# A head's output held in one PSUM bank, copied first in its step, transposed two steps later; a third bank for the transposes

## What is computed

```python
for layer in range(DEPTH):                       # 2
    h = _rmsnorm(x, mix_norm_gain[layer])
    q, k, v, conv_in = split(h @ w_in[layer])
    attn = _dilated_attention(rope(norm(q)), rope(norm(k)), v)   # 8 heads
    u = silu(layernorm(causal_dwconv(a * sigmoid(g))))           # 31 taps, 512 channels
    x = x + concat([attn, u]) @ w_out[layer]
    x = x + ffn(rmsnorm(x))                      # two matrix products and 3 taps
```

## Time and profile before

| | us |
|---|---|
| median of 3 runs | 2470.47 (2468.65 to 2470.99) |
| the profiled execution | 2470.12 |
| its span, first to last instruction | 2467.8 |
| attention steps of layer 0 | about 251 to 411 of the span |
| attention steps of layer 1 | about 1477 to 1636 of the span |

### The profile page before, as it was taken

How to read it: one execution, slowest core, us unless ns; L and a number is a source line. 1 busy time by engine, 2 the same in 40 slices (tenths; PEclk the granted TensorE clock), 3 DMA queues, 4 the chain that set the end, 5 groups by cost and what they waited for, 6 DMA issues and landing times.

```text
span 2467.8 us, 30567 instructions
## 1 busy us (share of the span) xinstructions
PE 2396.0 (97%) x11672; PEld 1956.5 (79%) x11672; DVE 1575.8 (64%) x1511; ACT 803.8 (33%) x1066; POOL 166.0 (7%) x57
## 2 busy tenths in 40 slices
PE   7999888999999999999999998899999999999999
PEld 6888667888888888888778876678888888888887
DVE  5999775566555555555749997746655555555555
ACT  4322665432222222222332237644322222222221
POOL 0222001100000000000103120011000000000000
PEclk9999999999999999999999999999999999999999
DMA  4334531111111111111112254301121111111111
GB/s 157 86 86 127 120 71 31 47 52 52 52 51 51 42 51 42 51 47 46 42 35 77 77 154 94 78 10 52 45 66 35 51 51 51 51 42 51 42 51 68
DMA packets 46674, 153.42 MB, mean 62 GB/s; under 512 B 7424, under 2 KB 10112, under 8 KB 46592
## 3 DMA queue, kind: packets, MB, share of 16 engines
q1 hardware_dynamic: 45728, 149.93, 21.1%
q10 hardware_dynamic: 864, 2.36, 0.2%
HBM read 131.02 MB, written 21.23 MB: 62 GB/s over the span
## 4 chain that ended last, share of the span: by engine, by line
PE 88%; issue 5%; DVE 4%; ACT 2%; POOLq 0%; DMA 0%; DVEq 0%; POOL 0%; SPq 0%; ACTq 0%
PE mm L436 59%; PE aux L436 19%; PE aux L572 3%; PE mm L548 3%; PE aux L591 3%; DVE y L1118 1%; DVE sc L1244 1%; PE aux L463 1%; ACT pT_large L882 0%; PE aux L472 0%; ACT sc L868 0%; DMA x<-xT 0%; POOLq L1421 0%; DVE x_lo L1060 0%; PE aux L529 0%
## 5 line engine op out<-in xcount | busy, mean ns | idle before, releaser
L436 PE MATMUL mm<-x_hi,w_hi 128*128 128x512 f32 x1952 | 609.3, 393 | 16.1 <-DVE x_lo L1060 11.6
L436 PE MATMUL mm<-x_hi,w_lo 128*128 128x512 f32 x1952 | 604.5, 391 | 0.0
L436 PE MATMUL mm<-x_lo,w_hi 128*128 128x512 f32 x1952 | 604.2, 391 | 0.0
L436 PEld LDWEIGHTS mm<-x_hi,w_hi 128*128 128x128 f32 x1952 | 363.9, 188 | 95.6 <-issue 11.9
L436 PEld LDWEIGHTS mm<-x_lo,w_hi 128*128 128x128 f32 x1952 | 367.0, 188 | 79.6
L436 PEld LDWEIGHTS mm<-x_hi,w_lo 128*128 128x128 f32 x1952 | 367.0, 188 | 78.8
L735 ACT ACTIVATE w_hi<-w_raw 128x1024 fp32r<-128x1024 f32 x154 | 162.0, 1058 | 654.7 <-PE mm L436 458.1
L1118 DVE SCALAR_TENSOR_TENSOR y<-u_pad,cpar,y 128x1024 f32<-128x1024 f32 x240 | 313.3, 1338 | 3.4 <-ACT y L788 2.6
L1054 DVE TENSOR_TENSOR x<-x,aux 128x1024 f32<-128x1024 f32 x176 | 214.8, 1221 | 120.4 <-PE aux L436 109.9
L1048 DVE TENSOR_TENSOR w_lo<-w_raw,w_hi 128x1024 fp32r<-128x1024 f32 x154 | 192.5, 1256 | 54.5 <-ACT w_hi L735 50.2
L1066 DVE TENSOR_TENSOR uv<-mm,rinv 128x1024 f32<-128x1024 f32 x44 | 53.9, 1225 | 220.1 <-PE mm L436 219.9
(11 more groups left out here) (185 smaller groups left out, 2897.1 us busy)
## 6 DMA issues: line engine op xcount, KB each, us to landing
w_raw<-weights SPq DMA_DIRECT2D x188, 512.0 KB, 3.6
qk_scratch<-m SPq DMA_DIRECT2D x64, 128.0 KB, 2.1
qk_scratch<-o SPq DMA_DIRECT2D x64, 128.0 KB, 2.1
x_hi<-qk_scratch SPq DMA_DIRECT2D x32, 256.0 KB, 6.3
q_first<-qk_scratch SPq DMA_DIRECT2D x8, 512.0 KB, 4.8
k_hh_first<-qk_scratch SPq DMA_DIRECT2D x16, 256.0 KB, 6.3
k_ll_first<-qk_scratch SPq DMA_DIRECT2D x16, 256.0 KB, 6.9
x_hi<-qk_scratch SPq DMA_DIRECT2D x8, 512.0 KB, 4.7
```

What stands on the lines that cost most here:

```text
L436: last = pe.matmul(acc[:, cols], a, b[:, cols], start=start and n == 0, stop=stop and n == 2)
```

## The change

ScalarE's copy of a head's output stands first in step 8h + 11 and no longer last. The transpose back moves from step 8h + 12 to 8h + 14, and in its step it now stands behind the product with v. The "o" fills move from the steps 23 and 25 to 24 and 26. As the output is copied earlier, all heads can use one bank (`o_bank`, the upper half of `stat_s`), and the lower half joins the two banks of `stat_b` as a third for the transposes. So fill f goes to bank f % 3 and waits for fill f - 3. One step is added to the end, a quarter of the first output product moves with it, and the sum over the convolution's channels that follows now waits for all three banks before its first half.

```diff
-O_AT = 23
+O_AT = 24
+H_AT = 14
@@
-        if n >= 12 and (n - 12) % TB == 0 and n < STEPS + 12:
-            fills.append((n, "h", (n - 12) // TB, None, None))
+        if n >= H_AT and (n - H_AT) % TB == 0 and n < STEPS + H_AT:
+            fills.append((n, "h", (n - H_AT) // TB, None, None))
@@
+TURN_BANKS = 3
+BANK_FILLS = [len(range(b, PT, TURN_BANKS)) for b in range(TURN_BANKS)]
@@
+        turn_bank = [stat_b[:, 0:BANK], stat_b[:, BANK:], stat_s[:, 0:BANK]]
+        o_bank = stat_s[:, BANK:]
@@
+        def bank_read(l, f, after=0):
+            return at(l, BANK_FILLS[f % TURN_BANKS], f // TURN_BANKS + 1 + after)
@@ turn
-                    bank = stat_b[:, f % 2 * BANK:(f % 2 + 1) * BANK]
-                    pe.wait_ge(pt_read[f % 2], at(l, PT // 2, f // 2 + 1))
+                    bank = turn_bank[f % TURN_BANKS]
+                    pe.wait_ge(pt_read[f % TURN_BANKS], bank_read(l, f))
+                    if f == 2:
+                        pe.wait_ge(v_turned, at(l, PAIRS, PAIRS))
@@ attend
-                    if k == 0 and (l or h >= 2):
-                        pe.wait_ge(o_moved, at(l, HEADS, h - 1))
+                    if k == 0 and (l or h):
+                        pe.wait_ge(o_moved, at(l, HEADS, h))
@@ PE, a step
-                        if FILLS[f][0] == n and FILLS[f][1] in "ph":
+                        if FILLS[f][0] == n and FILLS[f][1] == "p":
                             turn(f)
                     ...
-                        if FILLS[f][0] == n and FILLS[f][1] == "o":
+                        if FILLS[f][0] == n and FILLS[f][1] in "ho":
                             turn(f)
@@ PE, behind the steps
                 pe.wait_ge(y_summed, at(l, CT - 1, CT - 1))
+                for bank in range(TURN_BANKS):
+                    pe.wait_ge(pt_read[bank], at(l, BANK_FILLS[bank], BANK_FILLS[bank] + 1))
                 for half in range(2):
-                    pe.wait_ge(pt_read[half], at(l, PT // 2, PT // 2 + 1))
@@ ACT, a step
+                    if n >= 11 and (n - 11) % TB == 0 and n < STEPS + 11:
+                        move_out((n - 11) // TB)
                     ...
                     if n < STEPS:
                         exps(n)
-                    if n >= 11 and (n - 11) % TB == 0:
-                        move_out((n - 11) // TB)
```

More of the change, by code:

```diff
@@ L76 @@
 STEPS = HEADS * TB
-O_AT = 23
+O_AT = 24
+H_AT = 14
 BLOCKS = (0, 6, 1, 7, 2, 4, 3, 5)
 ATTENDS = ((5, 0), (6, 3), (9, 1), (10, 2))
-LAST_STEP = STEPS + 10
+LAST_STEP = STEPS + 11
 DOWN = GROUPS * KT
@@ L141 @@
 PT = len(FILLS)
-assert PT % 2 == 0
+TURN_BANKS = 3
+BANK_FILLS = [len(range(b, PT, TURN_BANKS)) for b in range(TURN_BANKS)]
 LAST_FILL = [max(i for i, f in enumerate(FILLS) if f[1] == "p" and f[2] == n) for n in range(STEPS)]
@@ L284, in trunk @@
         pt_full = sem("pt_full"); o_moved = sem("o_moved")
-        pt_read = [sem(f"pt_read{i}") for i in range(2)]
+        pt_read = [sem(f"pt_read{i}") for i in range(TURN_BANKS)]
         step_done = sem("step_done")
@@ L580, in attend @@
                         pe.wait_ge(v_turned, at(l, PAIRS, PAIRS))
-                    if k == 0 and (l or h >= 2):
-                        pe.wait_ge(o_moved, at(l, HEADS, h - 1))
-                    for bank in range(2):
-                        fills = [f for f in range(LAST_FILL[h * TB + at_step - 3] + 1) if f % 2 == bank]
-                        pe.wait_ge(pt_read[bank], at(l, PT // 2, len(fills) + 1))
-                    cols = slice(hh * BANK + pair * P, hh * BANK + (pair + 1) * P)
+                    if k == 0 and (l or h):
+                        pe.wait_ge(o_moved, at(l, HEADS, h))
+                    last_fill = LAST_FILL[h * TB + at_step - 3]
+                    for f in range(max(0, last_fill + 1 - TURN_BANKS), last_fill + 1):
+                        pe.wait_ge(pt_read[f % TURN_BANKS], bank_read(l, f, 1))
+                    cols = slice(pair * P, (pair + 1) * P)
                     for kb in range(2 * pair + 2):
@@ L590, in attend @@
                             if kb <= 2 * pair + half:
-                                last = pe.matmul(stat_s[half * HEAD_DIM:(half + 1) * HEAD_DIM, cols],
+                                last = pe.matmul(o_bank[half * HEAD_DIM:(half + 1) * HEAD_DIM, cols],
                                                  vp[b][:, kb, hh * HEAD_DIM:(hh + 1) * HEAD_DIM],
@@ L611, in _ @@
                         out_part(0, 0, [0], 0)
-                    if n == STEPS + 5:
+                    if n == STEPS + 7:
                         out_part(0, 0, [1], 0)
@@ L723, in _ @@
             act.sem_inc(pt_read[0], 1)
+            act.sem_inc(pt_read[2], 1)
             for t in range(0, KT, 2):
@@ L882, in read_turn @@
                         act.activation(pT(which)[:, a:z, :], bank[:, 0:(z - a) * P].rearrange(
-                            "p (k q) -> p k q", q=P), ACT.Copy).then_inc(pt_read[f % 2], 1)
+                            "p (k q) -> p k q", q=P), ACT.Copy).then_inc(pt_read[f % TURN_BANKS], 1)
                     else:
@@ L886, in read_turn @@
                         act.activation(o_nat[:, a * 4:(a + 1) * 4, :], bank.rearrange("p (b c) -> p b c", c=P),
-                                       ACT.Copy).then_inc(pt_read[f % 2], 1)
+                                       ACT.Copy).then_inc(pt_read[f % TURN_BANKS], 1)
                 def move_out(h):
@@ L892, in move_out @@
                     act.wait_ge(o_read, at(l, HEADS, h + 1))
-                    act.activation(o_turned[h % 2], stat_s[:, h % 2 * BANK:(h % 2 + 1) * BANK], ACT.Copy
+                    act.activation(o_turned[h % 2], o_bank, ACT.Copy
                                    ).then_inc(o_moved, 1)
                 for n in range(LAST_STEP):
+                    if n >= 11 and (n - 11) % TB == 0 and n < STEPS + 11:
+                        move_out((n - 11) // TB)
                     for f in range(PT):
@@ L1251, in read_turn @@
                         return
-                    fills = [g for g in range(f + 1) if g % 2 == f % 2]
-                    dve.wait_ge(pt_read[f % 2], at(l, PT // 2, len(fills) + 1))
+                    dve.wait_ge(pt_read[f % TURN_BANKS], bank_read(l, f, 1))
                     out = (slice(None), which, slice(a * BANK, (a + 1) * BANK))
@@ L1265, in read_out @@
                     dve.tensor_tensor(o_nat[:, :, hh * HEAD_DIM:(hh + 1) * HEAD_DIM],
-                                      stat_b[:, f % 2 * BANK:(f % 2 + 1) * BANK].rearrange("p (b c) -> p b c", b=TB),
+                                      turn_bank[f % TURN_BANKS].rearrange("p (b c) -> p b c", b=TB),
                                       row_rec.unsqueeze(2).broadcast_to([P, TB, HEAD_DIM]),
                                       ALU.mult).then_inc(o_read, 1)
-                    dve.drain().then_inc(pt_read[f % 2], 1)
+                    dve.drain().then_inc(pt_read[f % TURN_BANKS], 1)
                 step_taps = list(STEP_TAPS)
@@ L1282, in _ @@
                             read_turn(f)
-                    if n >= 12 and (n - 12) % TB == 0:
-                        read_out((n - 12) // TB)
+                    if n >= H_AT and (n - H_AT) % TB == 0 and n < STEPS + H_AT:
+                        read_out((n - H_AT) // TB)
                 def out_add(u, parts=range(2)):
```

## The result

The changed kernel takes 2448.07 us in the median of four runs (2444.03 to 2449.60), the kernel before 2470.73 beside it. The ratio is 0.9907, with a 95% interval of 0.989 to 0.9924: faster by 0.9%, within the stated range, at the price of the first rival and not of the forecast of 2437. One execution among all the runs of this text, the fourth of `turn_late`, took 3154.33 us at a granted clock of 0.705 and is set aside.

The account below looks back on a forecast made before the run. TensorE, busy 97% of the span, was taken as the bound, with waits in attention. Per layer 14.9 + 4.1 - 3 x 0.5 - 0.6 = 16.9 us, 33.8 in two, from 2470.1: forecast 2437 us, range 2427 to 2453.

Parts of the forecast that it names:

- the first rival: Clock still falls at boundaries behind step 11, so 11.6 us of the gain is lost: 2449 us, chance 0.20.
- the case that I gave 0.60: The forecast itself: copy waits gone and clock full in the attention steps, 2437 us.
- The waits for the copy go: TensorE's 14 waits for the copy of a head's output, 28.2 us in both layers, were to vanish.
- Heads 1 to 6 save 14.9 us, less 1.5 of waits: Six stretches per layer fall from 119.4 to 104.5 us, less 0.5 us at each of three boundaries.
- A wait of 0.4 to 1.6 us behind step 11, counted as 0.5: TensorE's new wait for VectorE's mask at three boundaries per layer, priced at 0.5 us each.
- The clock stays full: Clock of 1.00 in all attention stretches, ending slow stretches whose price was put at about 11.6 us.
- The third bank costs nothing: Third transpose bank: no price and no gain counted; up to 6 us of gain kept for the range.
- The rule of the Trainium skill that I had set against the change: Short idle times between matmul groups can lower the clock; three banks no cure, cost as the slow stretches now.
- The division moves at no price: VectorE's division by row sums moves to step 14 (6) at no cost, at most 0.9 us per head.
- The last head saves 4.1 us: Last head's stretch of 18.26 us loses 1.6 us of wait and 2.5 of slow clock.
- The end loses 0.6 us: Channel sum now waits for the last bank in both halves: 0.6 us lost per layer, between 0 and 0.9.
- the second: Rival: waits return for mask or exponential at half the places, 14 us beside the clock's 11.6: 2462 us, chance 0.08.

Follow-up runs that it names:

- turn_late: Changed kernel with the copy put back last in its step, behind the exponential; late transpose back, late "o" fills and three banks kept: 2447.57 us, median of three runs.
- copy_first: Changed kernel with the transpose back at step 12 and "o" fills at 23 and 25 again; copy first and three banks kept: 2436.05 us.
- fill_wait: Changed kernel with twelve identity transposes added on TensorE at the three boundaries behind step 11 of each layer: 2441.32 us.
- pool_later: Changed kernel with GpSimd's last addition over the channels held until the "o" fills of the third pair are split: 2443.20 us.
- order_only: Changed kernel with two banks for the transposes and two halves for the outputs, as in the kernel before; new order kept: 2443.36 us.
- two_banks_xlo: order_only with VectorE's subtraction of each "o" fill put behind the next step's mask: 2434.50 us.
- copy_xlo_pool: copy_xlo with GpSimd's last addition held until the "o" fills of the third pair are split: 2428.01 us.
- xlo_late: Changed kernel with VectorE's subtraction of each "o" fill put behind the next step's mask: 2428.34 us.
- copy_xlo: copy_first with VectorE's subtraction of each "o" fill put behind the next step's mask: 2427.59 us.

## Why the prediction came out as it did

The range held and the sign was right. The number was 11 us too low, because the case that I gave 0.20 came in place of the one that I gave 0.60, and other terms were off on top. That this rival's own number, 2449, lies within 1 us of the result is partly luck. It stood for the clock alone, at 11.6 us; the clock took some 9 in the profiled execution, longer waits and a collision took some 7.6 more, and cheaper stretches gave 3 back. The steps, for one layer:

- *The waits for the copy go.* Right: 28.2 us to none. But I gave the change two reasons for it, and one would do (copy_first, turn_late).
- *Heads 1 to 6 save 14.9 us, less 1.5 of waits.* They took 119.4 us and take 111.3 (384.33 - 273.04): 8.1 saved, where 13.4 was the forecast. A stretch without "o" fills and at full clock is 16.50 us and not 17.02, so there my measure was too dear by 0.5. The miss lies in three other places.
- *A wait of 0.4 to 1.6 us behind step 11, counted as 0.5.* This is the step that failed. The wait was 1.82 us, with 0.39 behind it, and stretches with "o" fills took 18.92 us, not 17.80 or with the wait 18.3. I had the chain right (ScalarE's copies, the subtraction, the mask) and took nearly its lower end. Its own upper end, with ScalarE late by the exponential that stands ahead, was the one to take.
- *The clock stays full.* Wrong, and it follows from the step above. I argued that 1.79 us behind step 3 had not brought the clock down, so a shorter wait behind step 11 would not. But the wait was no shorter. Three falls of 1.5 us are 4.6 us a layer, against the 5.8 that I had the old ones at; fill_wait shows the price, and that the idle time at this place is the cause. The argument was weak in itself too: one place without a fall says little, since the same wait of 1.82 us had a fall behind it at some places of pool_later and none at others.
- *The third bank costs nothing.* In the median it did not hold. The bank gathered into one wait behind step 11 what two banks spread over several, and the clock's price was larger than the bank's gain (order_only: 4.7 us faster without it, with the reserve on the spread made there). Where the clock was full, the bank gained 6 us (two_banks_xlo), the upper end of what I had kept for the range. The 37.3 us that I set as its limit were for two thirds waits of weight loads; the matmuls' were 13.1. The rule of the Trainium skill that I had set against the change, "TensorE: Matmul & The Clock Gate", section "A second HAM failure mode: psum-queue depth-cycling", was right about the outcome for this kernel. It blames frequent small idle times between groups of matmuls. The runs agree in part: the clock fell behind waits of 0.26, 0.99 and 0.40 us at one place of copy_xlo_pool, but order_only, with several waits of 0.4 to 0.8 us, kept it in all of its attention steps, and the changed kernel lost it behind 1.82 and 0.39.
- *The division moves at no price.* Wrong by 0.5 to 0.8 us in a stretch without "o" fills, by copy_first; that it is the division is read from the rows. I had looked at how long the next mask had waited for TensorE, 1.22 us, and not at how long VectorE itself would wait for the transposes in their new place.
- *The last head saves 4.1 us.* 2.4 (18.26 to 15.84), again for the clock, at 0.89.
- *The end loses 0.6 us.* Right by the spans: at the last copy to `sin` layer 1 is ahead by 21.27 us (1636.70 against 1615.43), at the end of the span by 20.7.
- *The signs.* The sign of the first rival is there (0.91 in the fourth and sixth stretches), and that of the second too: the scores' waits for the mask are over 15 us, 42.5 in the view and 17.7 for the matmuls. The chain from the "o" copies over the subtraction to the mask was its mechanism. It did not cost the 14 us of its price, as the six waits of 1.82 us make 10.9, and 3 of these I had counted.
- *Not seen at all*: the subtraction beside GpSimd's addition, 2.0 us a layer.

So per layer the waits and the low clock took back 3 x 0.6 + 4.6 us, the collision 2.0, and the cheaper stretches gave 3 x 0.5: 6.9 us, where the sum was out by 6.5 (16.9 forecast, (2467.8 - 2447.1) / 2 = 10.35 measured).

## What to carry to other kernels

When a wait is taken out of an in-order ring, ask which wait is next and what stands ahead of its releaser. Here more than half of the waits that went came back at other places. A wait of under two microseconds can cost the clock and with it nearly as much again, and work put into it can be free. When a change has two parts that each remove the same wait, price them one by one: here one part alone (the copy first) gave 12 us more than both, a good part of it since the clock stayed full, and moving VectorE's subtraction behind a mask gave 20 us more than the change. A sum of waits over a line can hold those of weight loads; ask for the matmuls alone before using it as a price.

## What the runs showed of the hardware

Two kinds of VectorE operation with both inputs in SBUF were held up beside a GpSimd addition, which reads SBUF too. The subtraction took 2.65 us in place of 0.69 and ended 0.55 us behind the addition; in xlo_late another took 2.07 and ended 0.55 us behind its addition too. A tap of the convolution that began inside another addition took 2.06 in place of 1.28:

```profile
285.81 2.38 POOL L1449 TENSOR_TENSOR u_pad<-y 128x1024 f32<-128x1024 f32 x1 [63.95 <-DVE y L1131]
...
287.20 2.06 DVE L1131 SCALAR_TENSOR_TENSOR y<-u_pad,cpar,y 128x1024 f32<-128x1024 f32 x1
```

VectorE's division, with one input in PSUM, kept its 0.69 us beside GpSimd's addition at 317.18 us. The Trainium skill, "SBUF — State Buffer", section "Who interferes with whom", says that a VectorE instruction with two SBUF inputs contends with a GpSimd instruction that reads SBUF, and that one with at most one, outside the modes with two ports, does not; these rows agree.

The granted clock went to its lower level, 1.2 GHz, behind all six waits of 1.82 us (with 0.3 to 0.4 us more behind them) in the changed kernel, and behind three of the six in pool_later. It fell behind 0.26, 0.99 and 0.40 us at one place each in the profiled executions of copy_xlo and copy_xlo_pool. It did not fall in order_only, where the longest wait at this place was 0.85 us, nor when twelve transposes stood in the wait. One fall cost 1.5 us in a stretch of 16.5.
